# Unit-matrix products in the waits of the norms and of the differential attention of a two-block fp32 kernel

## The reference, cut to what matters

```python
def rmsnorm(x, g):
    inv = lax.rsqrt(jnp.mean(x * x, axis=-1, keepdims=True) + RMS_EPS)
    return x * inv * g
def layer_norm(x, g, b):
    mu = jnp.mean(x, axis=-1, keepdims=True)
    var = jnp.mean(jnp.square(x - mu), axis=-1, keepdims=True)
    return (x - mu) * lax.rsqrt(var + LN_EPS) * g + b
# block one: for each of two layers
x = x + mixer(rmsnorm(x, norm_mix_g[layer]))          # Fourier/convolution heads, then pooling
h = rmsnorm(x, norm_ffn_g[layer])
x = x + (silu(h @ w_gate) * (h @ w_up)) @ w_down
# then rmsnorm(x, final_g)
# block two: for each of two layers, with mod = silu(c) @ w_ada + b_ada
a = attention(x * (1 + sc1) + sh1)                    # windowed with a sink, then differential
x = layer_norm(alpha * x + g1 * a, ln1_g, ln1_b)
x = layer_norm(alpha * x + g2 * square(relu((x * (1 + sc2) + sh2) @ w1)) @ w2, ln2_g, ln2_b)
# differential attention, 8 heads: softmax(q0 k0) - lam * softmax(q1 k1), times v, then a norm per head
```

## Time and profile before

| what | value |
|---|---|
| median of three runs | 2970.89 us (2963.16 to 2975.26) |
| the profiled execution, own time | 2973.86 us |
| its span | 2972.1 us |
| mean granted TensorE clock in it | 0.952 |
| TensorE matmul busy | 2702.2 us, 91% |
| VectorE, ScalarE, GpSimd busy | 1322.8, 696.0, 1356.0 us |

### The profile page before, as it was taken

The page is one execution under the profiler, slowest core; times in us unless marked ns, Lnnn a source line. Parts: engine busy times, 40 slices in busy tenths (PEclk is TensorE's granted clock), DMA queues, the critical chain, the costliest instruction groups (busy, mean ns, idle before and its releaser), DMA issues.

```text
span 2972.1 us, 40380 instructions
## 1 busy us (share of the span) xinstructions
PE 2702.2 (91%) x14676; PEld 2174.0 (73%) x14676; DVE 1322.8 (45%) x1870; ACT 696.0 (23%) x1295; POOL 1356.0 (46%) x862
## 2 busy tenths in 40 slices
PE   7588999998999989889989999999778888999998
PEld 6366777777777767666768888888567767778886
DVE  7953222233222245444344444444756555354544
ACT  2022000022000013566220100000446455111102
POOL 7226555544555553133545343434433221486662
PEclk9799999999999999899989999999889998899999
DMA  5013444443444441000111212121001010122331
GB/s 186 24 50 118 145 141 141 141 141 116 146 144 141 141 128 57 29 1 0 41 39 57 64 56 64 56 64 57 29 29 42 28 42 14 64 92 92 95 96 57
DMA packets 67361, 235.46 MB, mean 79 GB/s; under 512 B 8144, under 2 KB 9552, under 8 KB 67152
## 3 DMA queue, kind: packets, MB, share of 16 engines
q1 hardware_dynamic: 65792, 233.64, 24.5%
q10 hardware_dynamic: 1488, 0.69, 0.1%
HBM read 232.21 MB, written 2.10 MB: 79 GB/s over the span
## 4 chain that ended last, share of the span: by engine, by line
PE 77%; DVE 9%; issue 6%; POOL 4%; ACT 3%; DMA 1%; DVEq 0%; SPq 0%; ACTq 0%; POOLq 0%
PE ps L527 61%; PE ps L970 2%; PE ps L868 2%; PE ps L667 2%; PE ps L942 1%; PE ps L852 1%; PE ps L992 1%; POOL X L504 1%; PE ps L837 1%; PE ps L645 1%; DVE X L1795 1%; PE ps L829 1%; DMA raw<-in_stream 1%; DVE q L1842 1%; DVE hlo L1785 1%
## 5 line engine op out<-in xcount | busy, mean ns | idle before, releaser
L400 POOL TENSOR_SCALAR whi<-raw 128x1024 fp32r<-128x1024 f32 x334 | 375.3, 1124 | 1321.8 <-DMA raw<-in_stream 1321.6
L402 POOL TENSOR_TENSOR wlo<-raw,whi 128x1024 fp32r<-128x1024 f32 x334 | 825.9, 2473 | 27.9
L527 PE MATMUL ps<-Ahi,whi 128*128 128x512 f32 (+1 forms) x2192 | 759.6, 377 | 78.2 <-DVE tmp L1689 24.6
L527 PE MATMUL ps<-Alo,whi 128*128 128x512 f32 (+1 forms) x2192 | 752.7, 374 | 0.0
L527 PE MATMUL ps<-Ahi,wlo 128*128 128x512 f32 (+1 forms) x2192 | 751.5, 373 | 0.0
L527 PEld LDWEIGHTS ps<-Ahi,whi 128*128 128x128 f32 x2192 | 391.4, 192 | 179.2 <-issue 33.6
L527 PEld LDWEIGHTS ps<-Ahi,wlo 128*128 128x128 f32 x2192 | 391.7, 192 | 73.7
L527 PEld LDWEIGHTS ps<-Alo,whi 128*128 128x128 f32 x2192 | 391.6, 192 | 69.7
L527 PE MATMUL ps<-hhi,whi 128*128 128x512 f32 x1120 | 378.2, 375 | 20.6 <-DVE X L1795 19.7
L527 PE MATMUL ps<-hhi,wlo 128*128 128x512 f32 x1120 | 373.1, 370 | 0.0
L527 PE MATMUL ps<-hlo,whi 128*128 128x512 f32 x1120 | 372.9, 370 | 0.0
(11 more groups left out here) (227 smaller groups left out, 2859.5 us busy)
## 6 DMA issues: line engine op xcount, KB each, us to landing
raw<-in_stream SPq DMA_DIRECT2D x430, 512.0 KB, 3.9
X<-in_xT SPq DMA_DIRECT2D x2, 1024.0 KB, 7.1
arena<-in_dft SPq DMA_DIRECT2D x1, 2048.0 KB, 17.6
out_xT<-X SPq DMA_DIRECT2D x2, 1024.0 KB, 4.3
X<-in_ctxT SPq DMA_DIRECT2D x1, 1024.0 KB, 19.7
vec<-in_vec SPq DMA_DIRECT2D x1, 364.5 KB, 8.2
arena<-in_fmap SPq DMA_DIRECT2D x1, 256.0 KB, 13.1
arena<-in_cosq ACTq DMA_DIRECT2D x1, 256.0 KB, 2.7
```

The source lines that it names most:

```text
L400: pool.tensor_scalar(whi[:, s, part], raw[:, s, part], 1.0, 1.0, ALU.mult, ALU.mult).then_inc(sem("w_hi"), 1)
L402: pool.tensor_tensor(wlo[:, s, part], raw[:, s, part], whi[:, s, part], ALU.subtract).then_inc(sem("w_split"), 1)
L527: mm = pe.matmul(dst[c], w[:, b % RING, off:off + P], rhs(k, part, c0, n), start=(k == 0 and w is whi and part == 0), stop=(k == kn - 1 an ...
```

## The change

TensorE gets a helper that multiplies the unit matrix by itself n times, 128 columns, into a PSUM bank. It is called in every norm but n1 after the last sum (9 products) and after the spread (12), in every layer norm also after the spread of the mean (9), all into bank 6; and once in each pass of the differential attention, between the first two values and the wait for `qkB_lo` (18), into the first 128 columns of bank 0, with two waits on `sB_free` ahead of it. No other engine's program is touched.

```diff
+UNREAD = 6
@@ TensorE
+            def unread(bank, n):
+                for _ in range(n):
+                    pe.matmul(ps[:, bank, 0:P], ident[:, :], ident[:, :], start=True, stop=True, skip_group_check=True)
             def norm_squares(name, cols):
                 for k in range(KT):
                     pe.wait_ge(*when(f"{name}_sq", k + 1))
                     quarters(SQUARES[name], cols, tmp[:, k % 4, :], k).then_inc(sem(f"{name}_sum"), 1)
+                if name != "n1":
+                    unread(UNREAD, 9)
                 pe.wait_ge(*when(f"{name}_inv", 1))
                 spread(RSTD[name], cols, inv).then_inc(sem(f"{name}_rstd"), 1)
+                if name != "n1":
+                    unread(UNREAD, 12)
@@ the differential attention's pass
                 for t in range(V_FIRST):
                     values_of(t)
+                for t in range(2):
+                    pe.wait_ge(*when("sB_free", 16 * st + t + 1))
+                unread(0, 18)
                 pe.wait_ge(*when("qkB_lo", 4 * st + 4))
```

## The result

The changed kernel takes 2974.78 us (median of 20 runs, 2969.01 to 2992.78) against 2969.81 us before (20 runs, 2963.16 to 2975.39). The ratio is 1.0024, 95% interval 1.0013 to 1.0034, so about 7 us more (5.0 by the two medians, since the runs after scatter upwards): less than the half per cent that was called no difference. The forecast (2977, no difference) held, and the sum of +6.1 us was near. The interval excludes a gain.

A forecast was written before the change was run, and what follows sets the result against it. TensorE, busy 91% of the span, was taken to bound the kernel; terms summed to +6.1 us on the profiled 2973.86, so 2980.0, and 2977 after 3.0 off for the runs' median: no difference, range 2964 to 2991.

The forecast's parts named there:

- The price of one product: Each added TensorE instruction, two per product, takes 0.113 us at full clock and 0.227 at half.
- n4: Norm n4: added products delay L667 and the load behind it on the chain that sets the end; +1.8 us.
- Passes 1 to 3: Differential attention: products delay the first scores, 12.2 us against 3.0 of cover, nothing takes it back; +9.2 us.
- Pass 0: Attention's first pass: 4.1 us of products fit inside a wait of 8.4, little clock gain; -0.3 us.
- n2: Norm n2: products fit in a 2.24 us wait, and GpSimd's last split covers the modulation delay; 0.
- n5: Norm n5: first products vanish in 12 us of waiting, later ones may speed half-clock projections; -0.3 us.
- l2: Layer norm l2: spread gains at most 1.4 us, projections paced by VectorE give nothing; -0.8 us.
- l4: Layer norm l4: 9 products against a 1.55 us wait, spread already at full clock, last 12 free; +0.5 us.
- l1 and l3: Layer norms l1 and l3: products fill gaps, so spreads and half-clock projections behind run faster; -1.5 and -2.5 us.
- (a): Rival at all norm waits: added products do not hold the clock, all paid at half clock; +34 us, 3005; chance 0.11.
- (b): Rival: clock held everywhere and products cheaper than the head norm's; -9 us, 2962; chance 0.12.
- (c): Rival in the norms: gaps are refilled but the clock falls in what is left of them; 2982; chance 0.17.

The follow-up runs named there:

- e3: Changed kernel with only the attention's products, 36 instead of 18 in each pass, none in the norms; 2994.95 us, ratio 1.0078 to the kernel before.
- e5: e1 without the 12 products behind each spread; 2963.61 us, ratio 0.9978 to the kernel before.
- v3: e5 with VectorE's MLP sums waiting for GpSimd's residual tile by tile; 2956.53 us, ratio 0.9949 to the kernel before.
- e1: Changed kernel with the products of the norms alone, without the attention's 18 and their two waits; 2966.85 us, ratio 0.9990 to the kernel before.
- e4: e1 without the products of n2 and n4; 2966.06 us, ratio 0.9987 to the kernel before.
- r1: Kernel before with GpSimd's residual multiplication in l1 and l3 cut to 8 columns, the rest left out; 2964.17 us, ratio 0.9975.
- r2: e1 with GpSimd's residual multiplication in l1 and l3 cut to 8 columns, the rest left out; 2956.03 us, ratio 0.9955 to the kernel before.
- v1: Kernel before with VectorE's one wait for all eight residual tiles replaced by one per tile; 2961.93 us, ratio 0.9962.
- v2: e4 with VectorE's residual wait made tile by tile; 2952.30 us, ratio 0.9932 to the kernel before.
- e2: Changed kernel with the attention's products alone, none in the norms; 2982.18 us, ratio 1.0040 to the kernel before.

## Why the prediction was right, by its steps

**The price of one product: right.** Read from the head norm's unit-matrix products at 0.113 us full and 0.227 half. The 36 of a pass take 3.93 us to the next instruction's start, 0.109 each; the 18 behind n4's squares take 2.1 to the spread's start, 0.117. The Trainium skill's page "TensorE: Matmul & The Clock Gate", section "Back-to-back issue gap", has some 81 ns for a load and product of 128 columns in a stream. By that a pass would have paid 2.9 us (an estimate from the page's figure); the trace of these f32 products does not agree, and in e3 72 instructions in a row still start 0.111 us apart (7.96 us from the first to the scores).

**Passes 1 to 3: mechanism right, size near.** The delay at the scores is 8.4 us against 9.2 forecast, and nothing behind them takes it back within the pass. Two details differ. Pass 3's cover is not a fixed thing: the distance from values to scores is 2.7 us in before, e5 and v3, and 0.54 in e1, e4, r1, r2, v1 and v2, so in most executions the part costs 3 x 3.5 = 10.5 us, and 9.6 on the average of the nine without products (v3 has the 2.7 in pass 1 too). And in the changed kernel pass 3's values came 1.5 us sooner after pass 2 than before. That is the clock: in the projections ahead of pass 3 the kernel before ran at half clock from 2432.68 to 2439.51, 6.8 us, the changed one for 3.4 (2435.60 to 2439.02), and the difference falls from 2.80 to 1.28 in just these products. Why the stretch was shorter is not shown. The timed +11.9 (5.6 to 18.1 by its interval) is consistent with any of these.

**Pass 0: cost right, the rest open.** The products fit in the wait, as said, and with twice as many they still do (e3). The pass was 2.5 us shorter than before, but in other executions, with and without the products, it has between 4.4 and 13.0 us at half clock, and the least are e1's 4.8 and r2's 4.4, two kernels that have none of the products there. So no part of the 2.5 is put down to the change.

**n2, n4, n5, l2, l4: right within 0.7 us each.** (For l2 only up to its first projections: by pass 0 the difference is back where it was.) n4's load is issued later, as predicted, through L667 (L680 after); n2's is covered by GpSimd. n2's reading had a slip without effect: the first projections start at 237.95, behind an earlier split, and 246.2 is the end of the split ahead of the second group. The cover at the first is TensorE's wait of 5.6 us, of which 2.7 are left after. At n5 the gain of 1.7 us in the projections is given back where VectorE's tiles set the pace.

**l1 and l3: the mis-sized term.** The step read "6.1 us of projections at half clock, so up to -3.05" and "I take the projections in full". The clock did become full and the projections did gain. What failed is the unwritten assumption that nothing behind them keeps a pace of its own. The rows that would have said so stood in the trace of before: in l1 TensorE already waited 3.5 us for VectorE's first sum, and in l3 that sum was ready 0.04 us before TensorE came to it, so there was no time left for TensorE to come sooner. With the first sum on the path, l3 gives -0.7 and not -2.5, l1 -0.7 and not -1.5. Once the residual is out of the way, r1 to r2 and v1 to v2 gain 6 to 10 us, by ratios and medians, more than the 2.8 forecast for the norms. l1's other end showed too: its 9 products behind the squares ran at a clock of 0.62 and overhung, 3.28 us to the spread in place of 2.1.

**The rivals.** (a), that the products do not hold the clock, is refuted: clock 1.00 in the projections of l1 and l3, 45 us less work at half clock. (b), clock held everywhere and cheaper products, is refuted by the price. (c), that the clock falls in what is left of the gaps, is refuted for l1 and l3: behind the 12 products 1.71 us of gap remain in l1, and the clock is full after them.

That the sum came so near is partly luck. In the two profiled executions the 2.6 us of gain missing in l1 and l3 stand against 3.5 us more gain at n4, l2 and pass 0 (0.6, 0.65 and 2.2), of which pass 0's cannot be put down to the change. The norms' forecast of -2.8 stands against -1.7 in that pair and -3.0 in e1's runs, the attention's +8.9 against +11.9 in e2's; both gaps are within the intervals.

## What to carry to other kernels

A product that nobody reads pays in a wait that is longer than it, ahead of work that would run at half clock; ahead of work at full clock, with hardly any wait to fill, it costs nearly its whole price (3.5 of 4.06 us a pass). Before counting on a faster stretch, look at the next thing that the same engine needs from another one behind it, and at how long before its use it is ready: a wait, or readiness with nothing to spare as in l3, means that the gain ends there. That place may be the better edit: here one wait for eight tiles, made one per tile, gave 0.38% alone, and with it the same products gave 9.6 us by the medians where they had given 4.3.

## What the runs showed of the hardware that was not expected

- **Identical code in two lengths.** A pass of the attention takes 46.5 us from its first scores to its last value product with no half clock in it and some 51.0 us with 10.2 us of half clock; a few lie between (47.7 to 48.2 with 3.4, 49.4 with 6.8). Passes 1 to 3 were 46.5, 46.5 and 46.6 in the changed kernel; 51.1, 51.0 and 51.2 in e2, whose attention is the same; and 51.1, 46.5 and 46.5 in v2, which has no products there. No edit here is shown to decide which one comes. A step of 4.5 us that can come three times in an execution is larger than most terms of the forecast, and can make a large part of the spread of the runs: of the changed kernel's twenty, the six fastest (2969 to 2973 us) have a mean granted clock of 0.966 to 0.968 and the five slowest (2981 to 2993) one of 0.959 to 0.962.
- **A short run of products does not always raise the clock in time.** The 9 products behind l1's squares began with the clock at half (0.62 in the mean over them), while behind n4's and l3's squares the same 9 ran at full. What differs is the work ahead of them, and the runs do not say what in it decides.
- **An added line's busy time misleads.** 510 instructions show a mean of 282 ns each while they start 109 to 117 ns apart at full clock. Starts give the price.
